# A one-core fp32 block stack: running the sums before two post norms chunk by chunk, and taking one token tile's columns first in two units

## The reference, cut to what matters

```
x  = x + rmsnorm(xo @ w_xo, g_x_post)                 # first post norm
hf = rmsnorm(x, g_ffn_pre)
ff = (silu(hf @ w_gate) * (hf @ w_up)) @ w_down
x  = x + rmsnorm(ff, g_ffn_post)                      # second post norm
# next block: rmsnorm(x) @ even_w_in_2 (26 blocks of 128 columns and the gates)
```

## Time and profile before

| | |
|---|---|
| three runs, median | 1045.02 us (1044.1 to 1045.32) |
| profiled execution | 1042.93 us |
| its span, first to last instruction | 1040.8 us |
| PE busy | 1027.2 us (99% of the span) |
| DVE / ACT / GpSimd busy | 736.6 / 520.6 / 31.7 us |
| granted TensorE clock, mean | 0.999 of full speed |

### The profile page before, as it was taken

One profiled execution on the slowest core, in us unless ns is written; L12 is line 12 of the kernel. 1 busy time (PEld: TensorE's weight loads), 2 busy tenths in 40 slices (PEclk: granted clock), 3 DMA queues, 4 the chain that ended last, 5 costly groups with the idle time before them and its releaser, 6 DMA issues.

```text
span 1040.8 us, 17117 instructions
## 1 busy us (share of the span) xinstructions
PE 1027.2 (99%) x6908; PEld 914.5 (88%) x6908; DVE 736.6 (71%) x946; ACT 520.6 (50%) x673; POOL 31.7 (3%) x49
## 2 busy tenths in 40 slices
PE   8999999999999999999999999999999999999997
PEld 7998898788888889999888888889999988888885
DVE  6987564568878545898768788646788767778842
ACT  6875474454344435865453443435543354443531
POOL 1000100000000001000000000001000100000000
PEclk9999999999999999999999999999999999999999
DMA  9834463255554746444235545655444235545531
GB/s 346 342 128 149 169 223 122 81 183 176 192 197 164 276 167 264 165 145 139 93 127 191 196 164 199 245 200 187 161 160 147 98 122 204 200 161 197 191 137 41
DMA packets 27292, 183.41 MB, mean 176 GB/s; under 512 B 3200, under 2 KB 3472, under 8 KB 6112
## 3 DMA queue, kind: packets, MB, share of 16 engines
q1 hardware_dynamic: 25056, 175.01, 47.2%
q0 software_dynamic: 1744, 7.16, 1.9%
q10 hardware_dynamic: 432, 0.37, 0.1%
HBM read 181.48 MB, written 1.05 MB: 175 GB/s over the span
## 4 chain that ended last, share of the span: by engine, by line
PE 94%; DVE 3%; ACT 2%; issue 1%; POOL 0%; DVEq 0%; ACTq 0%
PE GT L1770 12%; PE D L1770 11%; PE GT L1732 9%; PE GT L1734 9%; PE GT L1733 9%; PE D L1733 7%; PE D L1732 7%; PE D L1734 7%; PE GT L1768 5%; PE D L1768 5%; PE D L2443 1%; PE GT L1945 1%; DVE s_wlo L937 1%; PE GT L1774 1%; PE D L1774 1%
## 5 line engine op out<-in xcount | busy, mean ns | idle before, releaser
L937 DVE TENSOR_TENSOR s_wlo<-s_raw,s_whi 128x2048 fp32r<-128x2048 f32 x164 | 372.8, 2277 | 176.7 <-ACT s_whi L453 176.2
L453 ACT ACTIVATE s_whi<-s_raw 128x2048 fp32r<-128x2048 f32 x164 | 307.6, 1900 | 91.9 <-PE D L1734 68.7
L1770 PE MATMUL GT<-s_x,s_whi 128*128 128x512 f32 x528 | 162.1, 393 | 0.0
L1770 PE MATMUL D<-s_x,s_whi 128*128 128x512 f32 x480 | 146.9, 392 | 0.0
L1732 PE MATMUL D<-s_whi,s_hTh 128*128 128x512 f32 x264 | 102.9, 390 | 0.0
L1733 PE MATMUL D<-s_wlo,s_hTh 128*128 128x512 f32 x264 | 102.7, 389 | 0.0
L1734 PE MATMUL D<-s_whi,s_hTl 128*128 128x512 f32 x264 | 102.7, 389 | 0.0
L1732 PE MATMUL GT<-s_x,s_whi 128*128 128x256 f32 x352 | 99.6, 283 | 0.0
L1768 PEld LDWEIGHTS GT<-s_x,s_wlo 128*128 128x128 f32 x462 | 84.4, 188 | 16.9
L1734 PE MATMUL GT<-s_x,s_wlo 128*128 128x256 f32 x352 | 98.3, 279 | 0.0
L1733 PE MATMUL GT<-s_x,s_whi 128*128 128x256 f32 x352 | 98.2, 279 | 0.0
(11 more groups left out here) (385 smaller groups left out, 1735.2 us busy)
## 6 DMA issues: line engine op xcount, KB each, us to landing
s_raw<-in_stream SPq DMA_DIRECT2D x164, 1024.0 KB, 4.8
s_gb<-in_rows POOLq DMA_DIRECT2D x4, 512.0 KB, 4.2
s_xn<-in_x SPq DMA_DIRECT2D x2, 512.0 KB, 4.3
s_raw<-in_stream SPq DMA_DIRECT2D x4, 256.0 KB, 6.6
s_y<-in_mem POOLq DMA_DIRECT2D x1, 1024.0 KB, 10.1
s_w<-in_cmpw POOLq DMA_DIRECT2D x1, 1024.0 KB, 11.5
s_poolm<-in_poolm POOLq DMA_DIRECT2D x1, 768.0 KB, 11.7
s_retd<-in_retm POOLq DMA_DIRECT2D x1, 768.0 KB, 7.1
```

The costliest lines, as they stand in the source:

```text
L453: nc.scalar.activation(whi[:, u % RING, 0:n], raw[:, u % RING, 0:n], ACT.Copy)\
L937: nc.vector.tensor_tensor(wlo[:, u % RING, 0:n], raw[:, u % RING, 0:n], whi[:, u % RING, 0:n], ALU.subtract).then_inc(lo_ready, 1)
L1770: ins = nc.tensor.matmul(o[:, f, :], hi[:, kt, c[f]], x2[:, kt, :], start=kt == 0, stop=kt == KT - 1)
```

## The change

`last_sums` runs the last two units of xo and of dn together: chunk 0 of both, then chunk 1, 2, 3, so 12 matmuls per chunk and one chunk finished every 12; both units are counted done at the end. Inside chunk 3, behind its first three matmuls, it transposes tile 0 of the new x. `tile_hi` and `tile_lo` make high and low parts of one tile (128 x 128 each, eight of each per tile). `first_pair` takes the place of the first unit: for the two next units (gu0 and gu1, ev0 and ev1) it multiplies the high weights with tile 0, high and low columns in one matmul; then it transposes tile 1; then it does the same for tile 1, with the low weights for both tiles. `rb_spread` stands behind both units. `keep_clock` is gone. ev0 and ev1 now lie as two halves in two banks each, and `evac_wide` sums the halves and then multiplies with `rb`. `norm_banks` becomes D2, D3 at the first post norm and G0, G1 at the second. The other norms are as before.

```diff
+            def tile_hi(n, t):
+                for kt in range(KT):
+                    if kt % 4 == 0:
+                        if t == 0:
+                            act.wait_ge(sem("first_tr"), 2 * (n - 3) + kt // 4 + 1)
+                        else:
+                            act.wait_ge(sem("norm_tr"), 4 * n + kt // 2 + 2)
...
+                    nc.scalar.activation(xTh[:, kt, P * t:P * t + P], norm_banks(n)[kt // 4][:, col:col + P], ACT.Copy,
+                                         scale=gain(NORMS[n][0], kt))\
+                        .then_inc(sem("norm_hi" if t else "first_tile_hi"), 1)
...
             def norm(n, last, first):
                 norm_squares(n, xn, lambda c: chunk(y, c), NORMS[n][2], range(first))
-                norm_hi(n, xTh)
+                if n < 5:
+                    tile_hi(n, 1)
+                else:
+                    norm_hi(n, xTh)
...
                 for c in range(4):
+                    if n is not None and c == 3:
+                        tile_hi(n, 0)
                     wait_sum(act, ph, c)
...
+            def evac_wide(u, dst, src):
+                dve.wait_ge(unit_done, u + 1)
+                link(nc.vector.reduce_sum(dst, src.rearrange("p f (a s) -> p f s a", a=2), AX))
+                nc.vector.tensor_tensor(dst, dst, same_rows(rb[:], 2), ALU.mult).then_inc(bank_read[bank(u)], 1)
...
-                gained(2)
-                update(1)
+                if n is None:
+                    gained(2)
+                    update(1)
+                else:
+                    update(1)
+                    gained(2)
+                    tile_lo(n, 0)
...
             def first_queries():
                 dve.wait_ge(sem("rb_ready"), 2)
-                evac_scaled(u0, nqT[:, 0:2, :], DB[0])
+                evac_wide(u0, nqT[:, 0:2, :], DD[:, 0:2, :])
 
             norm_rest(4, BASE["dn0"] + DN - 1, first_queries)
-            evac_scaled(u0 + 1, nqT[:, 2:4, :])
+            evac_wide(u0 + 1, nqT[:, 2:4, :], GT[:, 2:4, :])
...
+            def last_sums(ph, n, read, ready):
...
+                for b, o in enumerate(sum_banks(ph)):
...
+                    for j in (last - 1, last):
...
+                        for kk in range(2):
+                            if b == 3 and j < last and kk == 1:
+                                chunk_transposes(n, 0)
+                                chunk_transposes(n, 1)
+                            k = 2 * j + kk
+                            ins = passes(o[:], (act_h[:, k, c], act_l[:, k, c]), (hi[:, kk, w], lo[:, kk, w]), False,
+                                         j == last and kk == 1)
+                    if b < 3:
+                        ins.then_inc(sem("sum_done"), 1)
+                ins.then_inc(unit_done, 2)
...
+            def first_pair(n, u, pair):
...
+                for k, o in enumerate(pair):
+                    wait_unit(u + k)
+                    for kt in range(KT):
+                        pe.wait_ge(sem("first_tile_lo"), KT * (n - 3) + kt + 1)
+                        high_weights(u + k, o, 0, kt, start=kt == 0, stop=False)
+                chunk_transposes(n, 2)
+                chunk_transposes(n, 3)
+                for k, o in enumerate(pair):
+                    lo = wlo[:, (u + k) % RING, :].rearrange("p (k n) -> p k n", k=KT)
+                    for kt in range(KT):
+                        pe.wait_ge(sem("xT_ready"), KT * n + kt + 1)
+                        high_weights(u + k, o, 1, kt, start=False, stop=False)
+                        for f in range(2):
+                            ins = nc.tensor.matmul(o[:, f, 0:S], lo[:, kt, P * f:P * f + P], xTh[:, kt, :], start=False,
+                                                   stop=kt == KT - 1)
+                    ins.then_inc(unit_done, 1)
...
             def boundary(n, u, o, first):
 
-                if n < 5:
-                    chunk_transposes(n, 0)
-
-                    keep_clock(norm_banks(n)[3], 2)
-                    chunk_transposes(n, 2)
                 chunk_transposes(n, 1)
...
+                        if i is None and q == 0 and f == 0:
+                            if c == 0:
+                                first_pair(n, u, gate_up_banks(0))
+                                rb_spread(n)
+                            continue
...
-            for j in range(1, 4):
-                pe.wait_ge(sem("x_lo"), j + 1)
-                sum_unit("xo", j)
+            pe.wait_ge(sem("x_lo"), 2)
+            sum_unit("xo", 1)
+            last_sums("xo", 3, "x_lo", 0)
...
-            first_columns(u0, 4)
+            first_pair(4, u0, (DD[:, 0:2, :], GT[:, 2:4, :]))
             rb_spread(4)
-            for j in range(1, 4):
+            for j in range(2, 4):
                 unit(u0 + j, columns)
```

More of the change, by code:

```diff
@@ L303, in norm_banks @@
                 return [DB[2], DB[3], TB[0], TB[1]]
+            if n in (3, 4):
+                return DB[2:4] if n == 3 else G
             ph = {3: "xo", 4: "dn0", 5: "eo", 6: "dn1", 7: "oo"}.get(n)
@@ L958, in mem_scaled, with tile_lo @@
                     .then_inc(sem("mem_scaled"), 1)
+            def tile_lo(n, t):
+                for kt in range(KT):
+                    c, col = slice(P * t, P * t + P), P * (kt % 4)
+                    if kt % 4 == 0:
+                        if t == 0:
+                            dve.wait_ge(sem("first_tile_hi"), KT * (n - 3) + kt + 4)
+                        else:
+                            dve.wait_ge(sem("norm_hi"), KT * n + kt + 4)
+                    nc.vector.scalar_tensor_tensor(
+                        xTl[:, kt, c], norm_banks(n)[kt // 4][:, col:col + P], gain(NORMS[n][0], kt), xTh[:, kt, c],
+                        ALU.mult, ALU.subtract)\
+                        .then_inc(sem("xT_ready" if t else "first_tile_lo"), 1)
             def norm_lo(n, dst_h, dst_l, kts=range(KT)):
@@ L977, in norm_rest @@
                 name = NORMS[n][1]
-                norm_lo(n, xTh, xTl)
+                if n < 5:
+                    tile_lo(n, 1)
+                else:
+                    norm_lo(n, xTh, xTl)
                 norm_mean(n, name, 0)
@@ L1894, in chunk_transposes @@
             def chunk_transposes(n, c):
[L1896 removed]
+                o, t, by_tile = norm_banks(n), c // 2, n in (3, 4)
                 pe.wait_ge(sem("x_part"), 4 * (NORMS[n][2] - 1) + c + 1)
                 for kt in range(4 * (c % 2), 4 * (c % 2) + 4):
[L1899 to L1900 removed]
+                    dst = o[kt // 4][:, P * (kt % 4):P * (kt % 4) + P] if by_tile else \
+                        o[kt // 2][:, S * (kt % 2) + P * t:S * (kt % 2) + P * t + P]
+                    ins = nc.tensor.transpose(dst, xn[:, t, P * kt:P * kt + P], ident)
@@ L1901, in chunk_transposes @@
                     if t == NT - 1 and kt % 2:
                         ins.then_inc(sem("norm_tr"), 1)
+                if by_tile and t == 0:
+                    ins.then_inc(sem("first_tr"), 1)
+            def last_sums(ph, n, read, ready):
+                last = N_OF[ph] - 1
+                act_h, act_l = (xTh, xTl) if ph == "xo" else (hTh, hTl)
+                for b, o in enumerate(sum_banks(ph)):
+                    c, w = slice(P * (b // 2), P * (b // 2) + P), slice(512 * (b % 2), 512 * (b % 2) + 512)
+                    for j in (last - 1, last):
+                        u = sum_at(ph, j)
+                        if b == 0:
+                            pe.wait_ge(sem(read), ready + j + 1)
+                            wait_unit(u)
+                        hi = whi[:, u % RING, :].rearrange("p (k n) -> p k n", k=2)
+                        lo = wlo[:, u % RING, :].rearrange("p (k n) -> p k n", k=2)
+                        for kk in range(2):
[8 more added lines that the diff above has]
+                ins.then_inc(unit_done, 2)
@@ new lines, in first_pair, with high_weights @@
+            def first_pair(n, u, pair):
+                def high_weights(u, o, t, kt, **flags):
+                    hi = whi[:, u % RING, :].rearrange("p (k n) -> p k n", k=KT)
+                    c = slice(P * t, P * t + P)
+                    tokens = x2[:, kt, :].rearrange("p (a s) -> p a s", a=2)[:, :, c]
+                    for f in range(2):
+                        ins = nc.tensor.matmul(o[:, f, :].rearrange("p (a s) -> p a s", a=2)[:, :, c],
+                                               hi[:, kt, P * f:P * f + P], tokens, **flags)
+                    return ins
+                for k, o in enumerate(pair):
[7 more added lines that the diff above has]
+                    lo = wlo[:, (u + k) % RING, :].rearrange("p (k n) -> p k n", k=KT)
+                    for kt in range(KT):
+                        pe.wait_ge(sem("xT_ready"), KT * n + kt + 1)
+                        high_weights(u + k, o, 1, kt, start=False, stop=False)
+                        for f in range(2):
+                            ins = nc.tensor.matmul(o[:, f, 0:S], lo[:, kt, P * f:P * f + P], xTh[:, kt, :], start=False,
```

(6 more changed lines are left out.)

17 lines of the change are left out of this document (8 added, 9 removed).

## The result

The changed kernel takes 1047.57 us (median of 8 runs, 1045.98 to 1050.38), the kernel before on the same chip 1043.99 us (median of 8, 1042.96 to 1045.32). The ratio is 1.004, with a 95% interval of 1.003 to 1.0049: slower by 3.1 to 5.1 us. The forecast was 1047.8 us in a range of 1044.9 to 1050.5, 2.75 us above the kernel before. The time lies in the range and the sign is right; the difference was 3.6 us, 0.8 more than forecast.

What follows compares the result with a forecast made beforehand. PE bounds the kernel (94% of the chain that ended last). Losses of 1.6 us at the first post norm and 1.15 at the second sum to 2.75, on 1045.0: 1047.8 us, range 1044.9 to 1050.5.

Steps and rivals of the forecast that it cites:

- Sums free PE at 202.95: First post norm: the last sums leave PE free at 202.95, from 202.01 plus 0.94 us of tile 0's transposes.
- I take 0: Both norms: matmuls taking two blocks of 128 columns cost nothing extra; bounds 0 and 7.7 us per norm.
- The wait before tile 1: First post norm: PE waits 1.37 us (1.1 to 1.8) for tile 1's parts; the second norm's sum repeats it.
- The spread: First post norm: root spread at 216.14 instead of 211.87, 4.27 us later, delaying ACT's copy and DVE's chain.
- PE at gu2: Behind the first post norm: PE starts gu2 at 216.4 instead of 217.66, 1.2 us ahead.
- The wait at gu4: Feed-forward part: gu4's low weights come at 227.9, wanted at 227.5, so PE waits 0.4 us.
- rival A: Both norms: DVE's chain and ev0's reading are in time, leaving gains of 1.2 + 1.5, 1042.3 us; chance 0.09.
- The step that was mis-sized: Down product: DVE's low weights, 2.70 us of lead before, make dn2 start late; a loss of 1.6 us.
- The second norm: Before ev2: PE waits 2.65 us for ev0's reading behind the later spread; ev2 starts 1.15 us later.
- The time above the profiled one: Whole kernel: the median of the runs lies 2.1 us above the profiled execution's 1042.93, giving a base of 1045.0.
- Rival B: Only one of the two norms' losses comes: 0 or +0.1 us, so 1045.1 us; chance 0.14.
- Rival C: PE's clock falls to 1.2 GHz after a rest; half a unit costs 2.8 us, about 1050.6; chance 0.15, dearer matmuls included.

## Why the prediction was right, and where its sum was off

The mechanism was right. The changed kernel is slower because the root's spread now has 96 matmuls ahead of it, DVE's chain starts that much later, and ev0 is read that much later; not because PE has more to do.

- Sums free PE at 202.95: tile 0's first matmul starts at 202.80, in a kernel that was 0.10 early. Right. The matmuls that move two blocks of 128 columns take 3.94 us for 32 with the last one's latency; the next unit stands 206.57 - 202.80 = 3.77 us behind, 0.118 each against 0.113 of the earlier trace rows. The step is the same 0.118 where they alternate with line 2000's, which move 256 columns in a row, so it isn't the two blocks that cost the 0.005. "I take 0" was right.
- The wait before tile 1: 1.37 forecast, 1.18 and 1.18 measured. ACT's 128 columns, which I put at 0.30, are 0.27 each, and DVE's 0.27 against my 0.28:

```profile
207.21 2.17 ACT L478 ACTIVATE s_x<-D,s_gains 128x128 fp32r<-128x128 f32 x8 [2.30 <-PE D L1945]
...
208.38 2.16 DVE L990 SCALAR_TENSOR_TENSOR s_x<-D,s_gains,s_x 128x128 fp32r<-128x128 f32 x8 [2.36 <-ACT s_x L478]
```

- The spread: 4.27 us later forecast, 4.56 measured, since 96 matmuls at 0.118 instead of 0.113 more than make up for the shorter wait. PE at gu2: 216.4 forecast, 216.56 measured. The wait at gu4: 0.4 forecast, 0.37 measured. Then 0.2 us per pass: from gu4 on PE is held to 11.32 us a pass, though the list of waits, which leaves out short ones, shows none of these. The "44" matmuls that rival A puts ahead of the old spread are in the code 34 at the first norm (14 of them of 512 columns) and 48 at the second; no sum uses them.
- **The step that was mis-sized** is "at dn2 it starts at 336.80 + 4.27 = 341.07 instead of 339.50". It asked only when DVE's low weights are ready. The same chain also reads the last up product out of D2 and D3, PE waits for that before dn0, and its lead was 1.96 us, not 2.70. The loss is 2.7 where I had 1.6, and dn2 starts 2.75 us late, not 1.6, without waiting for low weights. With that wait put later it is 1.8, which is the forecast's own 1.6, 0.1 for a chain later than forecast and 0.1 for the handover; and the delay alone, in the kernel before, costs what the lead of 1.96 says, to 0.01 us in the trace.
- The second norm: a wait of 2.65 forecast before ev2, 2.55 measured; 1.15 us lost by forecast, 1.3 by the trace. Right.
- Not foreseen and of the other sign: 0.9 us gained in the last output's landing. 2.7 + 1.3 - 0.9 = 3.1, and the two profiled executions differ by 1045.98 - 1042.93 = 3.05. That the forecast difference of 2.75 came so near is luck in part: the two norms cost 4.0.
- The time above the profiled one. I had put 2.1 us on top of it, from the three runs of before. In the runs side by side the kernel before stood 1.1 above its profile and the changed one 1.6 above. So that the predicted 1047.8 came out only 0.2 us off is luck: a difference that was 0.8 too small was added to a time that was 1.0 too high.

Rival A (the waits don't come) is out: the two kernels with both spreads early are what it described. Rival B is out: each norm alone is slower. Rival C has a part in it. Six of the changed kernel's eight runs have a mean granted clock of 0.995 to 0.997 and take 1047.1 to 1050.4 us, the two at 0.999 take 1045.98 and 1046.07. In the kernel before, 17 of the 66 runs that stood beside the experiments were under 0.998, and their medians are 1.6 to 2.0 us above the others'. In the other eleven kernels the count goes by the second norm: 49 of 68 runs under 0.998 where it is changed (the changed kernel's own eight among them), 10 of 28 where it isn't. So what I wrote as one possible fall after a pause, at 2.8 us, is a smaller fall in some executions of every kernel, and in more of them with this change. It is the likely reason why the medians differ by 3.6 and the profiled executions by 3.05, for in neither of these does the clock fall before PE's last matmul. (Behind that it falls in every profile, where it costs nothing.)

That the pauses do it is not shown. With the pauses ahead of tile 1 nearly filled and no wait before ev2, 8 of 9 runs were still low. The falls in the profiled executions lie at three places. Two are at the start (11.4 and 11.8 us). Two lie behind the wait before ev2: at 405.8, 0.1 us behind it, in the kernel with the second norm's change alone, and at 411.2, 1.1 us behind it, in the changed kernel with the wait at dn0 put later. Five lie between 434 and 442. Laid on the kernel before by their shifts these are all at 434.3 to 435.2, within 1 us of the end of a stretch in which PE's matmuls have 64 rows and move as little as 15 columns, and which the change doesn't touch (rows of the kernel before):

```profile
430.32 1.90 PE L2302 MATMUL D<-s_ksT,s_nqT 64*128 64x128 f32 x16
...
432.50 1.96 PE L2358 MATMUL GT<-s_kcm,s_nqT 64*128 64x15 f32 x32 [0.27 <-DVE s_vcm L1373]
434.39 0.39 PE L1732 MATMUL GT<-s_x,s_whi 128*128 128x256 f32 x1
```

The Trainium skill ("TensorE: Matmul & The Clock Gate", section "What's actually happening") says that the throttle is the default state and activity releases it. The falls behind the 2.55 us wait agree with that in two executions (mean clock 0.63 from 405 to 408 us in the one, 0.53 from 411 to 414 in the other); the profiles of the changed kernel and of the one with only the first spread early have the same wait and no fall. Why the clock falls at the place near 434, and why more often with this change, stays open.

## What to carry to other kernels

An engine that waits for nothing can still hand its lateness on. When a step is put ahead of a small one that starts another engine's chain, the price is the chain's delay less the smallest lead of any step of it, and every semaphore that the chain counts has to be asked, the readings that free a bank as well as the data. Of such an edit keep the part that fills the gap and put the small step earlier: here 32 matmuls earlier at both norms turned +3.6 us into -2.6, each with the 0.9 us of the landing in it.

## What the runs showed of the hardware

- The last output of 256 KB landed 3.6 us behind its issue where a packet of about 8 KB of instructions fell among the output's packets, and 2.7 us where none did: the first in both kernels with the old code (before, and the one with only the spread moved), the second in all ten with the new code. No kernel was made to move that packet alone, so the cause is argued from its place, not shown.
- A matmul whose 256 columns lie in two blocks of 128 costs 0.118 us, and so does one of 256 in a row beside it (line 2000); in the kernel before it was 0.113.
- ScalarE reads 128 columns of PSUM with a scale in 0.27 us, eight in 2.17, where 256 columns took 0.39.
- The granted clock falls to half for a few microseconds in some executions of one and the same program on a single core, and a fall near 434 us cost 1.5 us in each of five traces (in the changed kernel with identities the shift goes from +3.75 to +5.30 over it). At half the clock the matmuls of 256 columns behind ev2's start stand 0.213 us apart, against 0.118 at full rate (second norm only). Runs with a mean clock under 0.998 are longer than the others of the same kernel by 0.7 to 3.1 us, by medians.
